# A hybrid encoder step on one core: turned, two-part queries, keys and cache come out of the input projection instead of being made inside attention

## The reference, cut to what matters

```python
xn = _rmsnorm(h, g_attn)
parts = jnp.split(xn @ w_in, ...)            # 2820 columns: q, k, v of four groups, and 4 gate columns
a_out = _stick_breaking(aq, a_k, a_v, ...)    # group A, 4 heads of 64
b_out = sliding window, 4 query heads, 2 key heads, sinks and a position bias   # group B
c_out = _diff_attention(cq, c_k, c_v, ...)    # group C: two maps of 32 columns, bias
d_out = _forgetting_attention(dq, d_k, d_v, ...)  # group D: gates
h = h + o @ w_out
h = h + jnp.square(jax.nn.relu(hn @ w_up)) @ w_down
h = h + jax.nn.sigmoid(h @ w_ple_gate) * (p_l @ w_ple_proj)
```

## Time and profile before

| | us |
|---|---|
| median of 3 runs (2068.09 to 2095.45) | 2070.28 |
| the profiled execution | 2087.65 |
| its span | 2086.0 |
| input projection, first to last product | 13.6 to 314.7 |
| attention, to the first product of the output projection | 314.7 to 1014.4 |
| the rest, which the change does not touch | 1014.4 to 2086.0 |

### The profile page before, as it was taken

The page is one execution under the profiler, slowest core; times in us unless marked ns, Lnnn a source line. Parts: engine busy times, 40 slices in busy tenths (PEclk is TensorE's granted clock), DMA queues, the critical chain, the costliest instruction groups (busy, mean ns, idle before and its releaser), DMA issues. The chain is left out here.

```text
span 2086.0 us, 29729 instructions
## 1 busy us (share of the span) xinstructions
PE 1927.6 (92%) x10334; PEld 1694.7 (81%) x10334; DVE 938.8 (45%) x1826; ACT 693.5 (33%) x1474; POOL 88.9 (4%) x152
## 2 busy tenths in 40 slices
PE   7999994789998679999798999999999999999898
PEld 6888883677877577778687989899998989998686
DVE  4211125877375877767345333333333333333434
ACT  5211114654254655445223222222221212211326
POOL 0111100000000000000110000000000000000000
PEclk9999996898599779989899999999999999999999
DMA  5322324344122326222431111111111111110202
GB/s 176 104 91 88 85 74 79 77 113 79 29 58 57 54 70 136 48 58 61 163 111 46 41 41 41 44 49 53 49 49 43 41 41 41 41 41 20 86 28 94
DMA packets 189252, 140.94 MB, mean 68 GB/s; under 512 B 147588, under 2 KB 157508, under 8 KB 189096
## 3 DMA queue, kind: packets, MB, share of 16 engines
q1 hardware_dynamic: 160696, 99.73, 18.7%
q0 software_dynamic: 9728, 34.63, 4.8%
q10 hardware_dynamic: 18688, 4.72, 0.9%
HBM read 114.95 MB, written 32.35 MB: 71 GB/s over the span
## 5 line engine op out<-in xcount | busy, mean ns | idle before, releaser
L105 PE MATMUL up<-xt_hi,w_hi_even 128*128 128x384 f32 x768 | 258.1, 336 | 1.9 <-PEq L1285 1.9
L107 PE MATMUL up<-xt_hi,w_lo_even 128*128 128x384 f32 x768 | 257.7, 336 | 0.0
L106 PE MATMUL up<-xt_lo,w_hi_even 128*128 128x384 f32 x768 | 257.6, 335 | 0.0
L107 PE MATMUL down<-w_hi_odd_b,hidden_lo 128*128 128x512 f32 x576 | 224.5, 390 | 0.0
L106 PE MATMUL down<-w_lo_odd_b,hidden_hi 128*128 128x512 f32 x576 | 224.5, 390 | 0.0
L105 PE MATMUL down<-w_hi_odd_b,hidden_hi 128*128 128x512 f32 x576 | 224.0, 389 | 0.0
L1494 DVE TENSOR_TENSOR h_rows<-down,h_rows 128x1024 f32<-128x1024 f32 x72 | 88.2, 1225 | 235.3 <-PE down L107 235.3
L1459 ACT ACTIVATE hidden_rows<-up 128x384 f32<-128x384 f32 x96 | 47.3, 492 | 415.5 <-PE up L107 415.5
L1227 PE MATMUL outs<-v_rows,probs_turned 128*128 128x64 f32 x984 | 144.0, 295 | 14.2 <-DVE probs_turned L680 11.5
L1227 PEld LDWEIGHTS outs<-v_rows,probs_turned 128*128 128x128 f32 x984 | 138.5, 216 | 19.4 <-DVE head_out L1063 7.5
L1487 DVE TENSOR_TENSOR hidden_rows<-hidden_rows 128x384 f32<-128x384 f32 x96 | 53.6, 558 | 222.8 <-ACT hidden_rows L1459 222.8
(11 more groups left out here) (232 smaller groups left out, 3673.8 us busy)
## 6 DMA issues: line engine op xcount, KB each, us to landing
w_raw<-w_up SPq DMA_DIRECT2D x64, 256.0 KB, 3.0
w_raw<-w_down SPq DMA_DIRECT2D x64, 256.0 KB, 3.4
proj_rows<-proj_out POOLq DMA_DIRECT2D x54, 235.0 KB, 2.4
w_raw<-w_in SPq DMA_DIRECT2D x48, 235.0 KB, 2.7
k_rows<-proj_rows SPq DMA_DIRECT2D x16, 288.0 KB, 3.3
q_rows<-proj_rows SPq DMA_DIRECT2D x16, 288.0 KB, 4.1
v_rows<-proj_rows SPq DMA_DIRECT2D x16, 288.0 KB, 3.4
head_rows<-head_out ACTq DMA_DIRECT2D x16, 288.0 KB, 3.1
```

What stands on the lines that cost most here:

```text
L105: nc.tensor.matmul(out, xh, wh, start=first, stop=False)
L106: nc.tensor.matmul(out, xh, wl, start=False, stop=False)
L107: return nc.tensor.matmul(out, xl, wh, start=False, stop=last)
```

## The change

The input projection is cut anew. Values and the gate columns are still made as rows (block 0, 388 columns, and block 5, 512 columns), but queries and keys are made turned: the weights stand still and three row tiles pass (384 columns), for 15 pieces of 128 columns by 3 groups of tiles, 45 units. ScalarE writes a unit's high part (scaled, for queries), VectorE its low part, and GpSimd's queue stores both to `q_turned_*` and `k_turned_*` in DRAM. Keys are also turned back to rows for the outputs, and the cached keys are loaded, turned, split and stored to `k_cache_turned_*`: 104 transposes for the cache and 56 for the new keys. SyncE's queue, behind that same wait, now loads finished operands for a job: keys, queries "straight" and "crossed" (halves swapped), cached keys, new keys and two spreads of the sample's queries in runs of 16 numbers, then the values and the rest as before. All count on `job_in0` or `job_in1`. The chunks of `prep_chunks` are gone from all engines. The bias is split in two F32R parts (two more VectorE instructions), masks and the unit matrix are kept in F32R, and products that were widened to 256 columns have their own width.

```diff
-                            sp.wait_ge(q["twice"], at("twice", PREP[prep_chunks(job - 1)[-1]] + 1 if job else 0))
-                            sp.dma_start(kr[:, :, :], rows_of(K_COL[g], kvh)).then_inc(q["rows_k"], 16)
-                            sp.dma_start(qr[:, :, :], rows_of(Q_COL[g], h)).then_inc(q["rows_q"], 16)
-                            sp.dma_start(kc[:, 0:nb, :], cache_of(0)).then_inc(q["rows_c"], 16)
                             sp.wait_ge(q["o_full"], at("o_full", TILES * (job - 1)))
-                            sp.dma_start(vr[:, e, :, :], rows_of(V_COL[g], kvh)).then_inc(done, 16)
-                            sp.dma_start(vc[:, e, 0:nb, :], cache_of(vcol)).then_inc(done, 16)
+                            sp.dma_start(kt[:, e, :].bitcast(F32), keys_[:, 0:SEQ]).then_inc(done, 16)
+                            sp.dma_start(qt[0][:, e, :].bitcast(F32), own[:, 0:SEQ]).then_inc(done, 16)
+                            for to, of in crossed:
+                                src = q2[g][bass.ds(P * h + of.start, half), :]
+                                sp.dma_start(qt[1][to, e, :].bitcast(F32), src[:, 0:SEQ]).then_inc(done, 16)
+                            n = P * cached(g)
+                            sp.dma_start(ks[:, e, :, 0:n].bitcast(F32), by_sequence(kc2[g][bass.ds(P * kvh, P), :])).then_inc(done, 16)
+                            sp.dma_start(ks[:, e, :, n:n + DEC_S].bitcast(F32), by_sequence(keys_[:, SEQ:SEQ + P])).then_inc(done, 16)
+                            sp.dma_start(spread(0, e), by_sequence(own[:, SEQ:SEQ + P])).then_inc(done, 16)
+                            for to, of in crossed:
+                                src = q2[g][bass.ds(P * h + of.start, half), :]
+                                sp.dma_start(spread(1, e)[to], by_sequence(src[:, SEQ:SEQ + P])).then_inc(done, 16)
+                            sp.dma_start(vr[:, e, :, :], vrows[:, bass.ds(V_COL[g] + HD * kvh, HD)].rearrange("(t p) d -> p t d", p=P)).then_inc(done, 16)
+                            sp.dma_start(vc[:, e, 0:nb, :], cache[:, bass.ds(vcol + HD * kvh, HD)].rearrange("(s p) d -> p s d", p=P)).then_inc(done, 16)
...
                     def body(j):
-                        first = prep_chunks(0)
-                        for k in range(len(first) + 2):
-                            if k < len(first):
-                                twice(first[k])
-                            if k >= 2:
-                                prep(first[k - 2])
...
-                            if s < NT:
-                                for chunk in AFTER[s]:
-                                    twice(chunk)
...
+                        nc.vector.tensor_copy(bih[:, e, :], bi[:, e, :]).then_inc(q["bias_hi"], 1)
+                        dve.wait_ge(q["bias_hi"], at("bias_hi", k))
+                        nc.vector.tensor_tensor(bil[:, e, :], bi[:, e, :], bih[:, e, :], ALU.subtract).then_inc(q["bias_ready"], 1)
...
                     def scores(i):
                         if t == 0:
-                            own = [WHERE[c] for c in prep_chunks(job)]
-                            for n_ in sorted({n_ % 3: n_ for n_ in sorted(own)}.values()):
-                                wait_read(pe, n_)
+                            job_loaded(pe, job)
...
+                    for m, (blk, g, kind, pair, col, n) in enumerate(QK):
+                        unit = FIRST_QK + m
+                        bank_free(unit)
+                        out = M[unit % 3][:, 0:GT].rearrange("p (t c) -> p t c", t=3)
+                        for k in range(KD):
+                            if sum(u[0] == blk for u in QK[:m]) == 0:
+                                pe.wait_ge(w_lo, blk * SLOTS + k + 1)
+                            last = three(out, WH[blk % 2][:, k, col:col + P], WL[blk % 2][:, k, col:col + P],
+                                         XH[:, 3 * n:3 * n + 3, k, :], XL[:, 3 * n:3 * n + 3, k, :], k == 0, k == KD - 1)
+                        last.then_inc(mm_full, 1)
+                        for _ in TURNS[m]:
+                            turn_bank(x)
+                            x += 1
```

More of the change, by code:

```diff
@@ L256, in _ @@
+                    for x in range(CR):
+                        pool.wait_ge(st_c[x], 32 * len(range(x, caches_before(NTURN), CR)))
+                    pool.wait_ge(st_k, 32 * len(k_pieces()))
                 @block.scalar
@@ L307, in _ @@
+                    for t in range(TILES):
+                        if t == 4:
+                            gates()
+                        if t == 8:
+                            act.wait_ge(l_v, 2)
+                            nc.scalar.activation(lam[:, 2:4], lam[:, 0:2], ACT.Exp).then_inc(l_a, 1)
+                        values_hi(TILES + t, FIRST_V2 + t, 512)
                 @block.vector
@@ L510, in encoder @@
             NAMES = {
-                "rows_k": "load of a head's keys", "rows_q": "of its queries", "rows_c": "of its cached keys", "job_in0": "other loads of the even head", "job_in1": "loads of the odd head",
+                "job_in0": "loads of the even head", "job_in1": "loads of the odd head",
                 "turned": "PE: a bank of transposes is full",
@@ L522, in encoder @@
                 "f_gates": "D: the sample's gates, queries less keys", "f_ready": "D: with their mask", "f_scores": "D: scores with gates",
-                "twice": "VectorE: rows of keys or queries stand twice",
-                "prep_hi": "ScalarE: the high part of turned keys or queries",
                 "c_ready": "C: weights can be transposed",
@@ L530, in encoder @@
                 "n_rstd": "C: 1 / rms", "n_scaled": "C: outputs scaled by it", "n_done": "C: the head's output is normed",
-                "bias_near": "B, C: a head's near bias with its mask", "bias_ready": "B, C: a head's bias tiles",
+                "bias_near": "B: the negated sink; C: the sample's bias", "bias_sum": "B, C: a head's near bias with its mask",
+                "bias_hi": "B, C: its high part", "bias_ready": "B, C: a head's bias tiles",
                 "stored0": "an even head's output is stored", "stored1": "an odd head's",
@@ new lines, in body, with by_sequence, spread @@
+                            own = q2[g][bass.ds(P * h, P), :]
+                            keys_ = k2[g][bass.ds(P * kvh, P), :]
+                            crossed = [(slice(x, x + half), slice(y, y + half)) for z in range(0, P, 2 * half) for x, y in ((z, z + half), (z + half, z))]
+                            def by_sequence(ap):
+                                return ap.rearrange("p (b n) -> p b n", b=DEC_B)
+                            def spread(part, e):
+                                return by_sequence(qz[part][:, e, :].bitcast(F32))[:, :, 0:DEC_S]
```

595 lines of the change are left out of this document (335 added, 260 removed).

## The result

The changed kernel takes **2352.58 us** (median of 4 runs, 2341.87 to 2362.12), the kernel before 2082.86 beside it (2068.09 to 2105.26): a ratio of **1.1326, 95% interval 1.1225 to 1.1427**. I had forecast 2049, with 2100 as the upper end. The profiled execution takes 2358.47 us, of which its span is 2356.9.

| stretch | before | after | forecast of the difference | measured |
|---|---|---|---|---|
| projection, first to last product | 301.1 | 492.0 | +22 | **+190.9** |
| last product to first score | 28.0 | 29.4 | +4 | +1.4 |
| attention, last product to output projection | 699.7 | 778.5 | -43 | **+79** |
| of it: between the passes | 27.8 | 15.8 | -10.6 | -12.0 |
| the rest | 1071.6 | 1072.7 | 0 | +1 |

What follows compares the result with a forecast made beforehand. TensorE was taken to bound the projection and most B, C, D jobs, a chain of engines A. Terms -87 - 10.6 + 4 + 48 + 3 + 22 = -21 us took 2070.28 to 2049 us; range 1998 to 2100.

Steps and rivals of the forecast that it cites:

- between the passes: Between attention's two passes: job 8's chunks no longer stand ahead of its scores, -10.6 us.
- the projection's: Input projection: 160 new transposes cost 20 us, weights in three transfers 2; ScalarE and VectorE stay hidden; +22 us.
- rival 3: Projection: bound by its transfers, ScalarE waiting before a stage or cache buffer; at 180 GB/s +66 us, 2115; 10%.
- The late waits: Attention: operands of jobs 3, 4 and 7 land late in each pass, VectorE waits; 24 us a pass, +48.
- TensorE's level: Attention: TensorE stays at its lower clock over more of A, plus one stretch like job 4's; +25 us, 2074; 8%.
- the chunks of job 1: Attention, job 1 (A): removing seven chunks from a chain where VectorE is fullest gains 10 us.
- the rule: TensorE's clock: activity releases the throttle, idleness brings it back; job 4's row disagreed, such a stretch being 22 us.
- The price of narrow products: Attention: an F32R product of 128 columns costs 0.29 us at most, as a plain one; 0.058 the other end.
- rival 2: Attention: narrow F32R products are priced by columns, -36 us, of which waits eat some 10: 2023; 15%.
- ahead of attention: Between projection and first scores: loading 3.5 MB of operands takes 18 us where 15.0 went before, +4 in all.
- the chunks in D: Attention, D jobs: -6.5 us for the job that carries chunks (job 6), nothing for the other (job 7).
- Rival 4: Attention's loads: short 64-byte pieces cost double, the six waits grow; +20 us, 2069; 10%.

Runs made afterwards that it cites:

- e1: Changed kernel with stores of queries, keys and turned cache written to 128 consecutive DRAM rows, read by attention in the wrong order: 2199.0 us, last projection product at 333.8.
- e5: Changed kernel with each head's rows stored by a transfer of its own, to the same DRAM rows: 2206.5 us, last projection product at 366.6.
- e2: Changed kernel with the stores of queries, keys and turned cache issued from ScalarE's queue, one unit behind: 2553.1 us.
- e8: Changed kernel with plain-row stores, attention's loads made to fit, bias first and sample's loads last on own semaphores: 2109.2 us, 1.0146 of the kernel before.
- e9: e8 with a job's keys and queries issued once the scores of the job two before are in PSUM: 2070.7 us, repeated at 2088.4.
- e15: e9 with the sample's queries loaded in 512-byte rows and spread by GpSimd: 2078.3 us, 0.9948 of the kernel before.
- fillers: Unused identity transposes added ahead of tiles' transposes in some jobs: four on e8 2111.3 us, eight on e8 2119.9, four on e9 2079.4.
- e13: Changed kernel with the sample's queries loaded in 512-byte rows to one place, not in 64-byte pieces spread by sequence: 2349.1 us.
- e14: Changed kernel with neither turned cache nor cache values loaded from job 2 on: 2304.5 us.

## Why the prediction was wrong, step by step

- **The step that failed is the projection's: "ScalarE and VectorE stay hidden, as long as the stores keep up", +22.** They didn't, and for a reason that rival 3 had not priced: it compared bytes with 180 to 249 GB/s for all queues together. All queues together moved 129 GB/s with the engines half idle. e1 and e5 show the cause in the form of the store, e2 and the packets of the changed kernel that such a store takes 2 or 4 of 16 engines. With plain rows the term is +17 (e1), so products, transposes and splits were right. Rival 3 had the place right (ScalarE before a stage or a cache buffer), had 10%, and at its 180 GB/s had 66 us of the 169 that came on top of the +22. I had read the rates of the earlier trace rows from transfers whose two sides both begin with 128 rows, and never asked whether the new destination begins so. This is 172 of the 270 us.
- **The late waits, +48: right in place and kind, too small.** Job 3's loads leave at 627.49 and VectorE goes on at 647.98: 20.5 us for 3.05 MB, where I had 15.2 from 240 GB/s. Without the 2.5 us of landing that is 169 GB/s, under even the lower bound of 219. VectorE also came to the semaphore sooner than I had put it (6.2 us for 7.5). In place of 6.4, 8.7 and 8.7 us it waits 14.2, 18.7 and 10.9 at most (14.2, 16.0 and 10.5 in the first pass). Jobs 3 and 6 take 41.8 and 44.2 us, some 10 more than the forecast's 32 and 34. In job 3 the longer wait (16.0 us for 8.7) is 7 of the 10. In job 6 it is 2 of the 10: TensorE is busy for 33.2 us at a clock of 0.69, and in e8, where the wait is gone, for 24.8 at 0.94 with the same products. So a wait there costs its own length and the clock behind it, and what I had set against that (1.3 us off) was too kind. (The bounds of this term, 24 and 55, come out at 21 and 57 from its own numbers.)
- **TensorE's level, a case of 8% for 25 us.** Half of attention's error is this. The four C jobs take 253 us where the steps gave some 210 (in which the slow stretch of job 4 still stands), the long A jobs 46.6 and 47.1 for 36.6. In A it is the clock alone: job 1 took 46.60 us at 0.78 in the kernel before, takes 46.50 at 0.63 in the changed kernel, and in e5, whose attention has the same instructions, 38.2 at 0.77:

```profile
444.10:482.30 38.20, 30.45 (x199) 27.10 (x198) 27.47 (x47) 22.56 (x40) 1.61 (x3) 0.77 0.44 104
```

  At an equal clock the chunks of job 1 are worth 8.4 us of my 10. In C, TensorE is busy for 95% of job 4 and its clock is at 0.61. That a stall isn't what holds it down, as the rule was weighed against the earlier trace rows, fits these rows too as far as they go: over 120 us of jobs 4 and 5 with TensorE busy for 95% the clock did not recover. But some wait stands in job 3 in every kernel with the change, so none tests it. What holds C's clock down is **open**: neither shorter waits (e9, e15) nor fillers brought C back to the 0.93 of the earlier trace rows.
- **The price of narrow products was wrong in the other direction.** I took 0.29 us for a product of 128 columns in F32R. From e8, TensorE's timeline in job 15 at the upper level:

```profile
987.72 0.28 PE L1327 MATMUL scores<-k_turned,q_turned_straight 128*128 128x256 f32 x1
987.84 0.28 PE L1327 MATMUL scores<-k_turned,q_turned_crossed 128*128 128x256 f32 x1
987.96 0.22 PE L1330 MATMUL scores<-masks_rounded,ident_rounded 128*128 128x128 f32 x1
988.02 0.62 PE L1345 MATMUL turns<-cst,probs 128*128 128x128 f32 x4
```

  From start to start 256 columns are 0.12 us and 128 are 0.06: rival 2's price by columns. Its gain did not come in full. Jobs 2 and 10 of e9, with waits of 1 to 2 us left, take 16.8 and 15.5 us at clocks of 0.91 and 1.00: at most 1.6 under my 17.1, where rival 2 had 5 under it.
- **Right**: between the passes -12.0 for -10.6; ahead of attention +1.4 for +4; the chunks in D (e8: 26.0 and 25.1 us); the rest unchanged. Rival 4 isn't borne out: it gave +20 if short pieces cost double, and without those of the queries, two thirds of them, e13's six waits are 9.8 us shorter, attention 13.6.

## What to carry to other kernels

Before a new transfer is priced by its bytes, look at the first dimension on both sides: where one of them was 2 or 4 here, two or four engines of 16 carried it, and a share far under 1 with late landings is how the profile shows it. Moving work out of a loop into operands that are loaded finished trades engine time for bytes on a path with a deadline: put what the next engine needs first on a semaphore of its own, and release the buffers one by one. With these the changed kernel is level with the one before. The engine time that was saved was paid again: in e15 by 17.7 us more in the projection, by the waits left in jobs 3 and 11 (13.3 us), and most of all by TensorE's level, 259 us in the four C jobs for the 208 that their chunks' price alone would give.

## What the runs showed of the hardware

- Stores from ScalarE's queue to DRAM sides that begin with 2 had a DMA share of 0.13 and 50 GB/s, with 4 0.26 and 102 GB/s (e2). To 128 plain rows from GpSimd's queue 192 KB of queries landed in 2.4 us (e1), to `[2, 64, 384]` in 9.5.
- On GpSimd's queue a split store alone has two or four packets in flight, and several together reached 11; on ScalarE's all stores shared the same two engines (share 0.13 with four issued).
- The split form on GpSimd's queue puts some 22,000 packets under 512 bytes more into 270 us (29793 for 7305 in e1), with no such piece in the data.
- An engine's queue can stand for 4.6 us in one issue (SyncE in e13) and for 21 in four (ScalarE in e2) behind what it issued before: the time of an issue is then a price of the transfers ahead of it (0.58 us for the same transfer in e14, with one fewer ahead).
- Job 12 of C took 51.2 us at a clock of 0.93 with chunks beside it; without them the same products took 56.8 (job 4) to 72.3 us (job 12) at 0.68 to 0.50 (e9).
